# Expert weights in eight double slots of 2 MB instead of sixteen slots of 1 MB

## The chip, the cores and the metric

The kernel runs on one core of one Trainium2 chip. The metric is the device time of one execution in microseconds (us); lower is better. A difference of about 0.2% (2.8 us) is what a measurement of this kernel can tell from no change.

## The reference

One layer over 256 tokens of width 1024, all in float32. Three token mixers (a gated linear recurrence, a chunked mLSTM, a chunked gated delta rule) share one projection, are gated, summed and projected, and a layer norm follows. Then comes a mixture of 32 experts, of which each token uses four, and a second layer norm. The change touches the expert part alone:

```python
logits = (xf @ router_w + router_b).astype(jnp.float32)
top_val, top_idx = lax.top_k(logits, TOP_K)          # TOP_K = 4 of N_EXPERTS = 32
gate = jax.nn.softmax(top_val, axis=-1)
...
def expert_block(args):
    tok, e = args
    hdn = x_pad[tok] @ w1[e] + b1[e]                 # w1[e]: 1024 x 2048
    glu, lin = hdn[:, :D_FF], hdn[:, D_FF:]
    glu = jnp.minimum(glu, SWIGLU_LIMIT)
    lin = jnp.clip(lin, -SWIGLU_LIMIT, SWIGLU_LIMIT)
    act = glu * jax.nn.sigmoid(SWIGLU_ALPHA * glu) * (lin + 1.0)
    return act @ w2[e] + b2[e]                       # w2[e]: 1024 x 1024
...
x = layer_norm(DN_ALPHA * x + y, ln2_g[l], ln2_b[l])
```

Every expert's weights are read once: 32 experts of 12 MB, 384 MB in all.

## The kernel before, in words

The kernel has two stages. The first, about a third of the time, computes the mixers, the output projection, the first layer norm and the routing. Its weights come in tiles of up to 1 MB (rows of 1 KB) through three buffers; line 377 issues each when the tile three places ahead has been used (`full`, line 338). The end of that stream is, in this order: `br20`, `ga22`, `br21`, `ga23`, `br22`, `br23`, `wo0` to `wo3` (`ga` and `wo` tiles are 1 MB, these `br` tiles 0.5 MB).

The second stage walks over the experts in 16 pairs. One pair's weights are laid out in 24 chunks of 1 MB: 16 for the up projection (8 input blocks for each half `f` of the hidden width) and 8 for the down projection. A chunk is 128 partitions by 2048 floats, so a row of 8 KB for each partition, and holds both experts of the pair side by side. `pair` (line 795) issues for every chunk eight matmuls of 512 columns: `up` at line 818, `down` at line 836. Between chunks stand the biases (line 811), the scatter of the pair before into the accumulators (`scatter`, line 763), the gather of the next pair's tokens (`gather`, line 775), the gates (line 854) and the turning of the hidden values (line 827). At the end of a pair ScalarE copies the result out (line 1145), and the next pair's `scatter` adds it in. After the last pair a last `scatter`, the second layer norm and two stores follow.

The chunks live in 16 slots of 8 KB for each partition: 12 in `ring`, 4 in `mix` (`SLOT`, line 308). SyncE issues all loads, one after the other, in `load_chunk` (line 357). Each slot has a semaphore `chunk_in<slot>`, on which `chunk(c)` makes the tensor engine wait; the last matmul of a chunk raises `chunk_used`. `load_turn` (line 399) issues chunk n when chunk n - 16 has been used (the wait is at line 402). The first 16 chunks have no such wait: four go out between the last mixer weights (after `br20`, `ga22`, `br21`, `ga23`), eight right after `wo3`, and slots 12 to 15 after the last output projection (`wo11` full for two, moved for one) and after the second router product (`lgt1` full for the last).

Of the kernel before, what the change touches and what calls it, by code (L numbers as in the profile page):

```python
# [18 lines left out]
P = 128  # L19
S = 256  # L20
NT = S // P
D = 1024
# [8 lines left out]
NE, TOPK, FF = 32, 4, 1024  # L31
KF = FF // P
NPAIR = NE // 2
EC = 2 * KD + KF
SLOTS = 16
RSLOTS = 12
PB = 2
CAP = 64
ROUNDS = S // CAP
# [149 lines left out]
def layer_kernel(nc, x, w_in, lru_conv_w, lru_conv_b, lru_wa, lru_ba, lru_wx, lru_bx,  # L189
# [3 lines left out]
    uses, bank_total = bank_uses()  # L193
    stream = weight_stream()
    stream_at = {name: n for n, (name, _, _) in enumerate(stream)}

    def stream_value(n):

        return 16 * sum(2 if src == "lru" else 1 for _, src, _ in stream[n % WBUFS:n + 1:WBUFS])
# [3 lines left out]
    with ExitStack() as ctx:  # L203
        sems = {}

        def E(name):

            if name not in sems:
                sems[name] = ctx.enter_context(nc.semaphore("s_" + name))
            return sems[name]  # L210

        RING = ctx.enter_context(nc.sbuf_tensor("ring", [P, 96 * 256], F32))
        MIX = ctx.enter_context(nc.sbuf_tensor("mix", [P, 28400], F32))
# [3 lines left out]
        def area(base, kb, words):  # L217
            return base[:, int(kb * 256):int(kb * 256) + words]
# [86 lines left out]
        B1R = area(MIX, 72.25, 512)  # L305


        SLOT = [area(RING, 8 * n, 2048) for n in range(RSLOTS)] + [area(MIX, kb, 2048)
                                                                   for kb in (48.25, 56.25, 24, 32)]

        XE = [area(MIX, 4 * n, KD * P).rearrange("p (c n) -> p c n", c=KD) for n in range(PB)]
        GLU = area(MIX, 8, 512)
# [25 lines left out]
        def full(eng, name):  # L338

            bank, n = uses[name]  # L340
            eng.wait_ge(E(f"bank_full{bank}"), n)

        def moved(eng, name):

            bank, n = uses[name]
            eng.wait_ge(E(f"bank_free{bank}"), n)
# [4 lines left out]

        @block.sync
        def _(sp):
            def load_chunk(n, pair):

                src = expert_w[bass.ds(pair, 1), n % EC].rearrange("e p n -> p (e n)")
                sp.dma_start(SLOT[n % SLOTS], src).then_inc(E(f"chunk_in{n % SLOTS}"), 16)  # L357


            ahead = [stream_at[name] for name in ("br20", "ga22", "br21", "ga23")]  # L360
            for t in range(NT):
                sp.dma_start(XTOK[:, t, :], x[0, t * P:(t + 1) * P, :]).then_inc(E(f"x_in{t}"), 16)
            for n, (name, src, col) in enumerate(stream):
                buf, loaded = WB[n % WBUFS], E(f"w_in{n % WBUFS}")
                if name == "wo3":
                    buf, loaded = WO3, E("wo3_in")
                    full(sp, "br03")
                elif n >= WBUFS:
                    full(sp, stream[n - WBUFS][0])
                if src == "lru":  # L370
                    both = buf.rearrange("p c n -> p (c n)").rearrange("p (k b n) -> p k b n", k=2, b=NB)
                    sp.dma_start(both[:, 0], lru_wa[0].rearrange("b i j -> i b j")).then_inc(loaded, 16)
                    sp.dma_start(both[:, 1], lru_wx[0].rearrange("b i j -> i b j")).then_inc(loaded, 16)
                    continue
                w = sources[src][0]
                k = w.shape[0] // P
                sp.dma_start(buf[:, 0:k, :], w[:, col:col + GW].rearrange("(c p) n -> p c n", p=P)
                             ).then_inc(loaded, 16)
                if name == "gq1":

                    sp.wait_ge(E("small_zero"), 4)
                    for q, (first, cols) in enumerate(((C_MI, MH), (C_MI + MH, MH), (C_GA, GH), (C_GA + GH, GH))):
                        sp.dma_start(WSM[:, :, 32 * q:32 * q + cols], w_in[0, :, first:first + cols]
                                      .rearrange("(c p) n -> p c n", p=P)).then_inc(E("wsm_in"), 16)
                if n == ahead[0]:
                    for event in ("ha_ready", "hb_ready", "hc_ready"):
                        sp.wait_ge(E(event), 1)
                if n in ahead:
                    load_chunk(ahead.index(n), 0)
            for n in range(len(ahead), RSLOTS):  # L390
                load_chunk(n, 0)
            full(sp, "wo11")
            load_chunk(RSLOTS, 0)
            load_chunk(RSLOTS + 1, 0)
            moved(sp, "wo11")
            load_chunk(RSLOTS + 2, 0)
            full(sp, "lgt1")
            load_chunk(RSLOTS + 3, 0)
            def load_turn(turn, pair, first=0):

                for n in range(first, PB * EC):
                    sp.wait_ge(E("chunk_used"), turn * PB * EC + n - SLOTS + 1)
                    load_chunk(n, pair + n // EC)
            load_turn(0, 0, SLOTS)
            with sp.Fori(1, NPAIR // PB) as q:
                load_turn(q, q * PB)
            sp.wait_ge(E("rounds_ready"), 1)
            rounds = sp.value_load(NR[0:1, 0:1], min_val=1, max_val=ROUNDS)
            with sp.If(rounds > 1):
                with sp.Fori(1, rounds) as r:  # L410
                    with sp.Fori(0, NPAIR // PB) as q:
                        load_turn(r * (NPAIR // PB) + q, q * PB)
            for t in range(NT):
                sp.wait_ge(E("out_ready"), t + 1)
                sp.dma_start(out[0, t * P:(t + 1) * P, :], X1[:, t, :]).then_inc(E("stored"), 16)
            sp.wait_ge(E("stored"), 16 * NT)
# [30 lines left out]
        def _(pe):  # L447
# [349 lines left out]
            def pair(turn, j):  # L797
# [4 lines left out]
                def chunk(c):  # L802

                    n = j * EC + c
                    pe.wait_ge(E(f"chunk_in{n % SLOTS}"), 16 * (PB * EC // SLOTS) * turn + 16 * (n // SLOTS) + 16)
                    return SLOT[n % SLOTS]

                def bias(f, bank):
                    for g in range(2):
# [4 lines left out]
                def up(f, c, bank):  # L814
                    w = chunk(f * KD + c)
                    for g in range(2):
                        for a in range(2):
                            ins = mm(PS[64 * a:64 * a + 64, bank + g, :], XE[j][:, c, 64 * a:64 * a + 64],  # L818
                                     w[:, a * D + g * 512:a * D + g * 512 + 512], start=False, stop=(c == KD - 1),
                                     skip_group_check=True)  # L820
                    ins.then_inc(E("chunk_used"), 1)
# [10 lines left out]
                def down(c, bank):  # L832
                    w = chunk(2 * KD + c)
                    for h in range(2):
                        for a in range(2):
                            ins = mm(PS[64 * a:64 * a + 64, bank + h, :], HT[:, c // 4, c % 4, 64 * a:64 * a + 64],  # L836
                                     w[:, a * D + h * 512:a * D + h * 512 + 512], start=(c == 0), stop=(c == KF - 1),
                                     skip_group_check=True)
                    ins.then_inc(E("chunk_used"), 1)
# [842 lines left out]

def expert_layout(w1, w2, b1):

    up = w1[0].reshape(NPAIR, 2, KD, P, 2, 2, 512).transpose(0, 5, 2, 3, 1, 4, 6).reshape(NPAIR, 2 * KD, P, 2 * D)
    down = w2[0].reshape(NPAIR, 2, KF, P, D).transpose(0, 2, 3, 1, 4).reshape(NPAIR, KF, P, 2 * D)
    return np.concatenate([up, down], 1), b1[0].reshape(NE, 4, 512).transpose(1, 0, 2).reshape(4 * NE, 512)


# [17 lines left out]
```

## Time and profile before

| | us |
|---|---|
| median of 3 runs (1422.99 to 1423.6) | 1423.18 |
| the profiled execution | 1421.26 |
| its span, first to last instruction | 1419.5 |
| TensorE busy (share of the span) | 1347.7 (95%) |
| VectorE, ScalarE, GpSimd busy | 358.6, 181.8, 7.4 |
| moved by DMA | 458.42 MB, 323 GB/s over the span |

The profile covers one execution. Times in it count from its first instruction. Its page divides the span into 40 slices of 35.5 us and shows for each how busy the engines and the 16 DMA engines were. MB and GB/s in the profile are decimal; an expert chunk is 1,048,576 bytes. TensorE's busy time counts pipelined matmuls and does not tell by itself that TensorE is the limit. "SPq" is SyncE's instruction queue, where DMAs are issued; a duration there is the time until the issuing instruction was done, not the transfer's.

### The profile page before, as it was taken

How to read it: one execution, taken by the hardware profiler on the slowest of the kernel's cores; microseconds unless marked ns; L12 is line 12 of the kernel's file. 1: busy time of each engine (PE TensorE's matmuls, PEld its weight loads, DVE VectorE, ACT ScalarE, POOL GpSimd, SP SyncE). 2: the span in 40 equal slices, each digit the busy share in tenths (PEclk: the TensorE clock that was granted, in tenths of full speed). 3: DMA queues.
4: the chain of work that ended last, by engine and by line, in shares of the span. 5: the costliest groups of instructions: out<-in, count | busy, mean ns of one | idle time of the engine just before them, and what ended most of it. 6: DMA issues, size and time to landing. Idle time of an engine off the chain costs nothing.

```text
span 1419.5 us, 19162 instructions
## 1 busy us (share of the span) xinstructions
PE 1347.7 (95%) x7864; PEld 749.0 (53%) x7864; DVE 358.6 (25%) x738; ACT 181.8 (13%) x278; POOL 7.4 (1%) x19
## 2 busy tenths in 40 slices
PE   8999999999999999999999899898999989999895
PEld 7889889988888534434434233332333324333241
DVE  4845667212114220120120110201102011120103
ACT  1331251101100200100100010010010001001000
POOL 1000000000000000000000000000000000000000
PEclk9999999999999999999999999999999999999999
DMA  7433222233579799999999999999999999999995
GB/s 216 148 119 89 60 90 60 90 118 104 178 269 365 261 411 421 421 421 422 422 422 422 422 422 422 422 422 422 422 422 422 422 422 422 422 422 422 422 422 215
DMA packets 112530, 458.42 MB, mean 323 GB/s; under 512 B 12633, under 2 KB 62029, under 8 KB 63341
## 3 DMA queue, kind: packets, MB, share of 16 engines
q1 hardware_dynamic: 110016, 454.16, 80.2%
q10 hardware_dynamic: 2476, 3.75, 0.8%
q8 instruction: 26, 0.43, 0.1%
q14 instruction: 12, 0.09, 0.0%
HBM read 456.83 MB, written 1.05 MB: 323 GB/s over the span
## 4 chain that ended last, share of the span: by engine, by line
PE 51%; DMA 24%; SPq 20%; DVE 3%; issue 2%; ACT 0%; DVEq 0%
SPq L357 20%; PE ps L471 19%; DMA ring<-expert_w 19%; PE ps L818 10%; PE ps L489 6%; PE ps L836 6%; DMA mix<-expert_w 4%; PE ps L775 2%; PE ps L763 2%; PE ps L811 2%; PE ps L710 1%; PE ps L481 1%; DMA mix<-w_out 1%; DMA mix<-w_in 1%; PE ps L827 0%
## 5 line engine op out<-in xcount | busy, mean ns | idle before, releaser
L818 PE MATMUL ps<-ring,mix 128*64 128x512 f32 x1536 | 343.1, 592 | 2.4 <-DMA ring<-expert_w 2.4
L471 PE MATMUL ps<-mix 128*128 128x256 f32 x1280 | 281.5, 380 | 1.0 <-DMA mix<-w_in 1.0
L471 PEld LDWEIGHTS ps<-mix 128*128 128x128 f32 x1280 | 241.5, 190 | 35.2 <-issue 2.9
L818 PEld LDWEIGHTS ps<-ring,mix 128*64 128x64 f32 x1536 | 108.6, 137 | 210.3 <-issue 192.5
L836 PE MATMUL ps<-ring,mix 128*64 128x512 f32 x768 | 181.4, 599 | 31.4 <-DMA ring<-expert_w 31.3
L1645 DVE TENSOR_SCALAR mix<-ps 128x512 f32<-128x512 f32 x32 | 22.1, 692 | 539.5 <-PE ps L818 539.5
L836 PEld LDWEIGHTS ps<-ring,mix 128*64 128x64 f32 x768 | 50.4, 136 | 149.1 <-issue 83.1
L818 PE MATMUL ps<-mix 128*64 128x512 f32 x512 | 116.4, 593 | 2.0 <-DMA mix<-expert_w 2.0
L1654 DVE COPY mix<-ps 128x512 f32<-128x512 f32 x32 | 22.1, 692 | 239.2 <-PE ps L827 239.2
L836 PE MATMUL ps<-mix 128*64 128x512 f32 x256 | 60.6, 601 | 12.5 <-DMA mix<-expert_w 12.5
L818 PEld LDWEIGHTS ps<-mix 128*64 128x64 f32 x512 | 35.2, 137 | 63.3 <-issue 53.7
L775 PEld LDWEIGHTS ps<-mix 128*64 128x64 f32 x1088 | 61.9, 138 | 11.0 <-issue 9.1
L775 PE MATMUL ps<-mix 128*64 128x128 f32 x1088 | 65.9, 275 | 0.5 <-DVEq L1630 0.5
L1143 ACT ACTIVATE mix<-mix 128x512 f32<-128x512 f32 x32 | 20.2, 630 | 332.2 <-DVE mix L1645 332.2
L489 PE MATMUL ps<-ring 128*128 128x128 f32 (+2 forms) x512 | 62.6, 281 | 0.0
L763 PE MATMUL ps<-mix 128*64 128x512 f32 x272 | 61.3, 592 | 1.1 <-ACT mix L1145 1.1
L489 PEld LDWEIGHTS ps<-ring 128*128 128x128 f32 x512 | 61.3, 192 | 1.3
L811 PE MATMUL ps<-mix 128*64 128x512 f32 x256 | 60.4, 592 | 0.0
L1145 ACT COPY mix<-ps 128x1024 f32<-128x1024 f32 x16 | 16.2, 1012 | 274.1 <-PE ps L836 274.1
L836 PEld LDWEIGHTS ps<-mix 128*64 128x64 f32 x256 | 16.8, 136 | 55.9 <-issue 30.8
L763 PEld LDWEIGHTS ps<-mix 128*64 128x64 f32 x272 | 19.4, 137 | 40.3 <-issue 38.3
L827 PEld LDWEIGHTS ps<-mix 128*64 128x64 f32 x512 | 30.2, 137 | 18.3 <-issue 18.3
(252 smaller groups left out, 779.7 us busy)
## 6 DMA issues: line engine op xcount, KB each, us to landing
ring<-expert_w SPq DMA_DIRECT2D x288, 1024.0 KB, 26.4
mix<-expert_w SPq DMA_DIRECT2D x96, 1024.0 KB, 27.4
mix<-w_in SPq DMA_DIRECT2D x34, 1024.0 KB, 5.3
mix<-w_br_lru SPq DMA_DIRECT2D x4, 1024.0 KB, 5.2
mix<-w_out SPq DMA_DIRECT2D x4, 1024.0 KB, 5.7
mix<-w_br_ml SPq DMA_DIRECT2D x4, 512.0 KB, 3.4
mix<-w_br_gd SPq DMA_DIRECT2D x4, 512.0 KB, 5.4
mix<-x SPq DMA_DIRECT2D x2, 512.0 KB, 5.5
```

Of the source, the lines that this page charges most:

```text
L357: sp.dma_start(SLOT[n % SLOTS], src).then_inc(E(f"chunk_in{n % SLOTS}"), 16)
L471: ins = mm(o[:, m * S:(m + 1) * S], w[:, c, m * P:(m + 1) * P], rhs[:, c, :], start=(m == 0 and c == 0), stop=(c == nk - 1), skip_group_ch ...
L489: ins = mm(o[0:lhs.shape[-1], lo:hi], lhs, rhs, start=True, stop=True, skip_group_check=True)
L763: ins = mm(PS[64 * a:64 * a + 64, 4 + 2 * t + h, :], GTS[:, t * P + 64 * a:t * P + 64 * a + 64], YS[:, h * 512:(h + 1) * 512], start=False ...
L775: ins = mm(PS[64 * a:64 * a + 64, bank, c * P:(c + 1) * P], X1[:, t, k:k + 64], ONE[:, t, :], start=(c == 0 and t == 0), stop=(t == NT - 1 ...
L811: mm(PS[64 * a:64 * a + 64, bank + g, :], PICK[:, 2 * g + f, a, :], B1R, start=True, stop=False, skip_group_check=True)
L818: ins = mm(PS[64 * a:64 * a + 64, bank + g, :], XE[j][:, c, 64 * a:64 * a + 64], w[:, a * D + g * 512:a * D + g * 512 + 512], start=False, ...
L827: ins = mm(PS[64 * a:64 * a + 64, bank, c * P:(c + 1) * P], HID[:, c * P + 64 * a:c * P + 64 * a + 64], ident, start=True, stop=True, skip ...
L836: ins = mm(PS[64 * a:64 * a + 64, bank + h, :], HT[:, c // 4, c % 4, 64 * a:64 * a + 64], w[:, a * D + h * 512:a * D + h * 512 + 512], sta ...
L1143: A(SIG, GLU, ACT.Sigmoid, scale=SWIGLU).then_inc(E("sig_ready"), 1)
L1645: ts(GLU, PS[:, bank, :], LIMIT, None, ALU.min).then_inc(E("glu_ready"), 1)
L1654: nc_v.tensor_copy(HT[:, n[1], :, :], PS[:, bank, :].rearrange("p (q n) -> p q n", q=4)).then_inc(E("ht_ready"), 1)
```

## The change

The 24 chunks of a pair are laid out in DRAM as 12 steps of two: a step is 128 partitions by 4096 floats, a row of 16 KB for each partition, in which the two chunks stand behind each other. One DMA of 2 MB loads a step. There are eight slots of 16 KB for each partition in the same memory: six in `ring`, and two in `mix` that lie where the four single ones lay. One semaphore belongs to each double slot. TensorE waits for a step at each of its two chunks and reads its half of the slot. SyncE issues step n when both chunks of step n - 8 have been used. Of the first eight steps, one goes out after `br20`, one after `br21`, four after `wo3`, one when `wo11` is full, and the last when `lgt1` is full. All arithmetic stays as it was.

```diff
+STEPS = 2
-SLOTS = 16
-RSLOTS = 12
+SLOTS = 8
+RSLOTS = 6
...
-        SLOT = [area(RING, 8 * n, 2048) for n in range(RSLOTS)] + [area(MIX, kb, 2048)
-                                                                   for kb in (48.25, 56.25, 24, 32)]
+        SLOT = [area(RING, 16 * n, 4096) for n in range(RSLOTS)] + [area(MIX, kb, 4096) for kb in (48.25, 24)]
...
-            def load_chunk(n, pair):
-
-                src = expert_w[bass.ds(pair, 1), n % EC].rearrange("e p n -> p (e n)")
-                sp.dma_start(SLOT[n % SLOTS], src).then_inc(E(f"chunk_in{n % SLOTS}"), 16)
+            def load_steps(n, pair):
+
+                src = expert_w[bass.ds(pair, 1), n % (EC // STEPS)].rearrange("e p n -> p (e n)")
+                sp.dma_start(SLOT[n % SLOTS], src).then_inc(E(f"steps_in{n % SLOTS}"), 16)
...
-                if n in ahead:
-                    load_chunk(ahead.index(n), 0)
-            for n in range(len(ahead), RSLOTS):
-                load_chunk(n, 0)
+                if n in ahead[::STEPS]:
+                    load_steps(ahead.index(n) // STEPS, 0)
+            for n in range(len(ahead) // STEPS, RSLOTS):
+                load_steps(n, 0)
             full(sp, "wo11")
-            load_chunk(RSLOTS, 0)
-            load_chunk(RSLOTS + 1, 0)
+            load_steps(RSLOTS, 0)
             moved(sp, "wo11")
-            load_chunk(RSLOTS + 2, 0)
             full(sp, "lgt1")
-            load_chunk(RSLOTS + 3, 0)
+            load_steps(RSLOTS + 1, 0)
             def load_turn(turn, pair, first=0):
 
-                for n in range(first, PB * EC):
-                    sp.wait_ge(E("chunk_used"), turn * PB * EC + n - SLOTS + 1)
-                    load_chunk(n, pair + n // EC)
+                for n in range(first, PB * EC // STEPS):
+                    sp.wait_ge(E("chunk_used"), turn * PB * EC + STEPS * (n - SLOTS + 1))
+                    load_steps(n, pair + n // (EC // STEPS))
...
-                    pe.wait_ge(E(f"chunk_in{n % SLOTS}"), 16 * (PB * EC // SLOTS) * turn + 16 * (n // SLOTS) + 16)
-                    return SLOT[n % SLOTS]
+                    m = n // STEPS
+                    pe.wait_ge(E(f"steps_in{m % SLOTS}"),
+                               16 * (PB * EC // STEPS // SLOTS) * turn + 16 * (m // SLOTS) + 16)
+                    return SLOT[m % SLOTS][:, 2 * D * (n % STEPS):2 * D * (n % STEPS + 1)]
...
-    return np.concatenate([up, down], 1), b1[0].reshape(NE, 4, 512).transpose(1, 0, 2).reshape(4 * NE, 512)
+    steps = np.concatenate([up, down], 1).reshape(NPAIR, EC // STEPS, STEPS, P, 2 * D).transpose(0, 1, 3, 2, 4)
+    return (steps.reshape(NPAIR, EC // STEPS, P, STEPS * 2 * D),
+            b1[0].reshape(NE, 4, 512).transpose(1, 0, 2).reshape(4 * NE, 512))
```

## Rows read from the trace of the kernel before

**Rows 1.** The page, part 2: DMA engines, busy tenths and GB/s in 40 slices; packets.
```profile
DMA  7433222233579799999999999999999999999995
GB/s 216 148 119 89 60 90 60 90 118 104 178 269 365 261 411 421 421 421 422 422 422 422 422 422 422 422 422 422 422 422 422 422 422 422 422 422 422 422 422 215
DMA packets 112530, 458.42 MB, mean 323 GB/s; under 512 B 12633, under 2 KB 62029, under 8 KB 63341
```

**Rows 2.** Lines of TensorE: 500 to 690 us, then 900 to 1300 us (busy, mean | idle before).
```profile
L836 PE MATMUL ps<-ring,mix 128*64 128x512 f32 x192 | 42.6, 592 | 0.0
...
L836 PE MATMUL ps<-ring,mix 128*64 128x512 f32 x320 | 77.1, 602 | 17.7 <-DMA ring<-expert_w 17.7
```

**Rows 3.** Chain, in order of time (start us, us, what), late in the stream.
```profile
1124.41 26.45 DMA ring<-expert_w
...
1153.58 5.99 SPq L357
...
1184.06 26.45 DMA ring<-expert_w
```

**Rows 4.** Windows: us, busy of PE, PEld, DVE, ACT, POOL, PEclk, DMA share, GB/s.
```profile
422.25:423.25 1.00, 1.00 (x6) 0.89 (x5) 0.57 (x1) 0.00 (x0) 0.00 (x0) 1.00 1.09 389
459.00:462.00 3.00, 1.72 (x13) 1.23 (x12) 2.54 (x9) 0.03 (x1) 0.00 (x0) 1.00 1.01 426
505.00:510.00 5.00, 5.00 (x30) 1.86 (x28) 0.00 (x0) 0.00 (x0) 0.00 (x0) 1.00 1.01 428
900.00:1000.00 100.00, 91.73 (x540) 34.43 (x540) 14.54 (x34) 8.40 (x11) 0.00 (x0) 1.00 1.01 422
```

**Rows 5.** DMA view, the one issue at 478.5 us, its time to landing alone.
```profile
ring<-expert_w SPq DMA_DIRECT2D x1, 1024.0 KB, 5.6
```

**Rows 6.** Timeline of SyncE's queue, 477 to 506 us: the first refills of the slots.
```profile
478.50 2.04 SPq L357 DMA_DIRECT2D ring<-expert_w  x2
...
485.37 2.04 SPq L357 DMA_DIRECT2D ring<-expert_w  x2
...
490.99 0.33 SPq L357 DMA_DIRECT2D ring<-expert_w  x1
...
494.45 3.76 SPq L357 DMA_DIRECT2D ring<-expert_w  x3
...
501.32 3.76 SPq L357 DMA_DIRECT2D ring<-expert_w  x3
```

**Rows 7.** Windows: the gap before the first refill and the stretch behind it.
```profile
472.00:479.00 7.00, 7.00 (x50) 3.17 (x48) 1.65 (x8) 2.35 (x4) 0.00 (x0) 1.00 0.01 2
479.50:500.00 20.50, 20.50 (x152) 9.53 (x150) 1.98 (x3) 3.46 (x5) 0.00 (x0) 1.00 0.89 321
```

**Rows 8.** Chain at the end: the last chunk's matmuls and the copy behind them.
```profile
1402.03 1.96 PE ps L836 x8
...
1404.01 1.02 ACT mix L1145
```

**Rows 9.** Timeline of SyncE's queue, 384 to 420 us: mixer weights and first chunks.
```profile
385.18 0.42 SPq L357 DMA_DIRECT2D ring<-expert_w  x1
391.59 0.37 SPq L377 DMA_DIRECT2D mix<-w_in  x1
...
401.95 0.37 SPq L377 DMA_DIRECT2D mix<-w_in  x1
408.86 3.82 SPq L377 DMA_DIRECT2D mix<-w_br_gd  x2
```

**Rows 10.** DMA view of the issues at 391.6 and 401.9 us: times to landing.
```profile
mix<-w_in SPq DMA_DIRECT2D x1, 1024.0 KB, 10.0
...
mix<-w_in SPq DMA_DIRECT2D x1, 1024.0 KB, 9.4
```

**Rows 11.** Chain, the first pair and the begin of the second, on TensorE.
```profile
474.88 1.87 PE ps L811 x8
...
520.19 8.58 PE ps L836 x40
528.77 1.72 PE ps L811 x8
```

## The prediction

> **What bounds the kernel now.** I read the slices first. The DMA engines are nine tenths busy or more from the fifteenth slice to the last but one, and from the sixteenth at 421 or 422 GB/s without a dent [rows 1]. So the question is whether TensorE waits for them. The lines view answers by stretch: from 500 to 690 us the down projection (line 836) never waits, in the 400 us from 900 it idles 17.7 us for `ring<-expert_w` [rows 2]. TensorE begins with a full set of slots, uses it up until about 700 us, and from then on runs at the pace of the stream. In the chain the same link comes back every 59.65 us (1184.06 - 1124.41), which is one pair, 24 chunks, so 2.485 us a chunk [rows 3]. A million bytes and a bit (1,048,576) in 2.485 us is 422 GB/s, the rate of the slices: nothing but the transfers sets this pace. The chain's pieces on "SPq L357", such as 5.99 us [rows 3], are the issuing instruction held up behind a full queue. They cost nothing, for the DMA share stays at 1.01 meanwhile [rows 4].
>
> So the end is: the moment from which the stream no longer pauses, plus the chunks left times the time of one, plus what follows the last landing. The change works on all three.
>
> **The rate of the stream.** A transfer of 128 rows over 16 engines gives each engine eight rows. At 1 KB rows the saturated rate is 389 GB/s [rows 4]; an engine moves a sixteenth of it, so a row takes 1024 / 24.3 = 42.1 ns. At 8 KB rows the best stretches reach 426 to 428 GB/s [rows 4]; at 427, an engine's 65,536 bytes of a chunk take 2456 ns. Let each row cost a fixed f besides its bytes, and the hand-over to the next transfer about the same f. Then 2456 = 9f + 64 x (42.1 - f), so f = 238 / 55 = 4.3 ns. A step of two chunks with 16 KB rows needs nine f where two chunks needed eighteen: 9 x 4.3 = 39 ns less, of 4970.
>
> In the long stretch a chunk takes 2485 ns, 29 ns more than in the best ones. No row tells whether this extra goes with the bytes (it stays, 58 ns a step) or with the rows (half goes, another 29 ns). The ends are a saving of 39 and of 68 ns a step. I take the middle, 53 ns, and keep both ends.
>
> How many steps count? 384 chunks less the 16 preloaded and the 8 of the start below: 360 chunks, 180 steps. The saving is 180 x 53 ns = 9.6 us, between 7.0 and 12.2.
>
> Here the Trainium skill speaks twice. A lone chunk takes 5.6 us to land [rows 5] but 2.485 us in the stream [rows 3]: the fixed part of a transfer lies beside other transfers. The Trainium skill, SBUF — State Buffer, section "The DMA setup-cost knee", says that each transfer pays roughly 2 us whatever its size. Read as serial cost it would give 192 transfers fewer, some 380 us; the trace disagrees, since nearly nothing of it is left in the stream. The Trainium skill, DMA: Bandwidth & Descriptors, section "Why small descriptors are slow", gives about 3 cycles a packet (3.5 ns at the 850 MHz stated there), where the rows give 4.3; by its figure the certain part of the saving is 180 x 9 x 3.5 ns = 5.7 us, an estimate, instead of 7.0.
>
> **The start: the first refills.** With all 16 chunks landed the DMA engines stand still from 472 to 479 us [rows 7] until TensorE has used a chunk. SyncE's queue shows the refills: 478.50 and 480.22 (two issues, 1.72 apart, the time of eight matmuls), 485.37 and 487.09, 490.99, 494.45 and 496.17 and 497.88, then 501.32 [rows 6]. Served one after the other at 2.49 us each they end at 480.99, 483.48, 487.86, 490.35, 493.48, 496.94, 499.43, 501.92 (all later by the same latency, which cancels); the next is there at 501.32, so no pause follows. A step goes out at the second of each two: 480.22, 487.09, 494.45, 497.88. At 4.97 us they end at 485.19, 492.06, 499.42, 504.39, and the next is issued at 503.04, in time. The stream falls into its steady run 2.5 us later. My sum draws the pauses of before somewhat too long (3.5 us, where a share of 0.89 against 1.01 over 20.5 us makes 2.4 [rows 7]), so 1.5 to 2.5 us; I take 2.5. TensorE does not wait for this: it holds 16 chunks until 700 us. But the stream never pauses again, so nothing gives the 2.5 us back.
>
> **The end.** Before, the last chunk's eight matmuls follow its landing at once: 1.96 us, then the copy at line 1145 [rows 8]. Now both chunks of the last step land together, and the last but one also runs after the landing. Chunks back to back take 8.58 / 5 = 1.72 us [rows 11]. That is +1.7 us. In the middle of the run it costs nothing, as two chunks (3.7 us) fit into the 4.97 us to the next step.
>
> **The mixers' end.** The second chunk now goes in front of `ga22` instead of behind it, and the fourth in front of `ga23`. `ga22` is issued at 391.59 and lands 10.0 us later, at 401.6 [rows 9, 10]; TensorE turns to it when `ga23` goes out, 401.95, the moment at which `br20` has been used. Only 0.35 us is spare. A chunk issued at 385.18 is through by about 390, so the double one ends around 392.7, just as `ga22` (391.6 plus about 1 us) begins to move: a delay of 0 to 0.3 us, under cover. `ga23` lands at 401.95 + 9.4 = 411.35; TensorE needs it at 412.3, when the last `br` tile of the pair at 408.86 goes out [rows 9]. In front of it stand the same bytes as before, two chunks. I cost both at nothing; if the cover fails, TensorE is the bound there and up to 0.5 us goes straight into the end. Slot 14's load moves from the moved `wo11` to the full `lgt1`, some 8 us later, but the engines stand idle at 472 us with everything landed [rows 7], and the chunk is used after 505 us. Nothing.
>
> **Edits with one answer.** Half the issues on SyncE: it is never what the stream waits for. Fewer descriptors: the queue was held up at 26.45 us from issue to landing [rows 3], some 10.6 chunks; eight steps stay within 16 MB, seven of which are under way or landed while one is used, and TensorE falls behind by at most the work between a pair's chunks, 53.9 - 24 x 1.72 = 12.6 us [rows 11], under three steps. The stream doesn't starve. TensorE's instructions are the same.
>
> **Sum.** -9.6 + 2.5 + 1.7 = -5.4 us, between -8.0 and -2.8, or -3.8 with the small start. The profiled execution took 1421.26, 1.8 over its span and 1.9 under the median of 1423.18; the change adds nothing outside the span, so the difference is set against the median: 1417.8.
>
> **Rivals.**
> *The extra vanishes.* The rate with 16 KB rows stays at its undisturbed best all along: 39 + 58 = 97 ns a step, -17.5 + 4.2 = -13.3 us, 1409.9. For it: whole stretches run at 428 [rows 4]. Against: they are short, and with a deep queue every slice reads 422 [rows 1]. 5%.
> *Nothing gained (just slower).* The change doesn't do what it says: the queue cuts a 16 KB row into two pieces, or the fixed 4.3 ns of a 1 KB row isn't there at 8 KB. Then at most the hand-over, 180 x 4.3 ns = 0.8 us, is saved, and the coarser grain costs its 4.2: +3.4 us, 1426.6. For it: no transfer of before has rows over 8 KB. 20%.
> *Longer rows collide more (slower).* The engines' rows lie twice as far apart in DRAM, 16 KB instead of 8. If the 29 ns extra a chunk is engines getting in each other's way, and it doubles for the same bytes, a step costs 58 - 39 = 19 ns more: +3.4 + 4.2 = +7.6 us, 1430.8. It decides from the point at which a step takes more than 4970 - 4200 / 180 = 4947 ns; every further 1% is 8.9 us. For it: the extra comes up with a deep queue; against: 8 KB rows suffer only 1.2%. 12%. [...]
> *A new wait at the mixers' end* eats the gain: 3%.
>
> **Chances.** The forecast has 60%, of which 12 points lie at the end where the extra stays, within 0.2%. 0.2% of 1423 is 2.8 us, about what a measurement of this kernel can tell from no change. Faster: 48 + 5 = 53%. Within: 12, 9 of the 20 of nothing gained (3.4 us is just past the line), and 3: 24%. Slower: 11 + 12 = 23%. The range runs from 1410 to 1428: it takes in both ends of the forecast and nothing gained, and leaves out most of the collisions and half of the vanishing extra. The forecast's own range is 1415.2 to 1420.4.
>
> **What the profile would show.** Packets fall from 112,530 [rows 1] by some 24,600 for the rows and 3,000 for the hand-overs, if rows aren't cut. The slices from the sixteenth on read 424 to 428 GB/s instead of 422, if the rate gains, and the chain comes back after 59.0 to 59.2 us. The first refill is issued near 480.2. At the end 16 matmuls of line 836 stand behind the last landing. No new idle before line 471 between 385 and 425 us. I am wrong if the slices read 422 or less, or if the start of the second stage moves.

## The result and the profile after

The changed kernel takes 1411.85 us (median of 4 runs, 1410.07 to 1414.87); the kernel before, on the same chips, 1423.39. The ratio is 0.9924, with a 95% interval of 0.9912 to 0.9936: 11.5 us faster, where 5.4 was forecast. The profiled execution took 1411.46 us, its span is 1409.7, 9.8 us less than before.

From the page of the changed kernel, part 2 as in [rows 1]:

```profile
DMA  7433121232579699999999999999999999999994
GB/s 217 149 120 90 60 90 61 90 119 90 171 272 354 242 399 427 428 428 430 428 429 429 427 430 428 429 429 427 429 429 429 428 428 430 428 428 429 427 430 200
DMA packets 84879, 458.39 MB, mean 325 GB/s; under 512 B 9560, under 2 KB 58956, under 8 KB 60268
```

The slices read 427 to 430 GB/s where they read 421 or 422. The packets are 27,651 fewer: the 24,576 rows and 3072 hand-overs that vanish if a 16 KB row goes in one piece, and three others. The page's DMA list gives 33.1 us for the landing of a 2 MB step in `ring`, from issue on; nothing waits for that number, as with the 26.4 us of before.

The chain late in the stream (start us, us, what), beside [rows 3]:

```profile
829.91 32.08 DMA ring<-expert_w
...
1064.86 32.05 DMA ring<-expert_w
...
1123.60 32.02 DMA mix<-expert_w
...
1182.30 32.02 DMA ring<-expert_w
```

The link now comes back once a pair, in turn in `ring` and in `mix`. Single links are 58.70 to 58.77 us apart; the six pairs from 829.91 to 1182.30 us take 352.39 us, 58.73 a pair, 4.894 us a step. Three pairs of before, from this link to the last of [rows 3], take 178.91 us, 59.64 a pair, 4.970 for the same bytes:

```profile
1005.15 26.44 DMA ring<-expert_w
```

TensorE still waits for the stream, in the same place as before (lines view, 900 to 1300 us, beside [rows 2]): the bound has not changed, only its pace.

```profile
L836 PE MATMUL ps<-ring,mix 128*64 128x512 f32 x320 | 74.3, 598 | 22.2 <-DMA ring<-expert_w 22.2
```

Where the 9.8 us of the span lie is read from two links of the chain: the first matmuls of the second stage and the copy after the last chunk. The first line stands in the stretch 472 to 482 us, the others at the end.

```profile
475.98 1.87 PE ps L811 x8
...
1358.45 32.04 DMA mix<-expert_w
...
1390.54 3.68 PE ps L836 x16
...
1394.24 1.02 ACT mix L1145
```

Before, these two stand at 474.88 and 1404.01 [rows 11, rows 8]. So the second stage, from its first bias matmul to the last copy, took 929.13 us and takes 918.26: 10.9 us less. It began 1.1 us later, and behind the copy both need the same 15.5 us. The start of the second stage moves from run to run for a reason of its own (below), so this length of the second stage is the sharper measure. It comes from one trace of each kernel; the changed kernel was profiled a second time, with 918.41 us.

### The profile page after: what moved, and what is told of

Same layout as the page of the kernel before. It is cut to its first block, busy times and chain, and to the rows that moved or that the text cites. A ratio compares the mean times of both kernels' runs of the same rounds, so it can differ in the third digit from the quotient of the medians.

```text
span 1409.7 us, 18467 instructions
## 1 busy us (share of the span) xinstructions
PE 1338.6 (95%) x7864; PEld 756.4 (54%) x7864; DVE 358.3 (25%) x738; ACT 181.8 (13%) x278; POOL 7.4 (1%) x19
## 4 chain that ended last, share of the span: by engine, by line
PE 68%; DMA 29%; DVE 3%; issue 0%; SPq 0%; ACT 0%; DVEq 0%
PE ps L818 20%; PE ps L469 19%; DMA mix<-expert_w 14%; DMA ring<-expert_w 14%; PE ps L836 7%; PE ps L487 6%; PE ps L773 4%; PE ps L761 4%; PE ps L811 2%; PE ps L708 1%; PE ps L479 1%; DMA mix<-w_out 1%; DMA mix<-w_in 1%; PE ps L854 0%; PE ps L827 0%
## 5 line engine op out<-in xcount | busy, mean ns | idle before, releaser
L818 PE MATMUL ps<-ring,mix 128*64 128x512 f32 x1536 | 341.9, 592 | 0.0
L818 PEld LDWEIGHTS ps<-ring,mix 128*64 128x64 f32 x1536 | 109.2, 137 | 205.8 <-issue 199.4
L836 PE MATMUL ps<-ring,mix 128*64 128x512 f32 x768 | 176.1, 596 | 38.0 <-DMA ring<-expert_w 38.0
L836 PEld LDWEIGHTS ps<-ring,mix 128*64 128x64 f32 x768 | 53.9, 137 | 146.9 <-issue 98.8
L818 PE MATMUL ps<-mix 128*64 128x512 f32 x512 | 115.4, 592 | 0.0
L773 PEld LDWEIGHTS ps<-mix 128*64 128x64 f32 x1088 | 62.7, 140 | 10.8 <-issue 9.1
L818 PEld LDWEIGHTS ps<-mix 128*64 128x64 f32 x512 | 35.7, 137 | 59.6 <-issue 57.9
L836 PE MATMUL ps<-mix 128*64 128x512 f32 x256 | 57.9, 596 | 9.6 <-DMA mix<-expert_w 9.6
L761 PE MATMUL ps<-mix 128*64 128x512 f32 x272 | 61.3, 592 | 1.1 <-ACT mix L1145 1.1
L811 PE MATMUL ps<-mix 128*64 128x512 f32 x256 | 60.4, 592 | 0.0
L836 PEld LDWEIGHTS ps<-mix 128*64 128x64 f32 x256 | 18.5, 137 | 48.7 <-issue 36.5
L761 PEld LDWEIGHTS ps<-mix 128*64 128x64 f32 x272 | 19.5, 137 | 40.2 <-issue 38.2
L827 PEld LDWEIGHTS ps<-mix 128*64 128x64 f32 x512 | 30.1, 137 | 18.3 <-issue 18.3
## 6 DMA issues: line engine op xcount, KB each, us to landing
ring<-expert_w SPq DMA_DIRECT2D x144, 2048.0 KB, 33.1
```

Of the source, the lines that this page charges most:

```text
L761: ins = mm(PS[64 * a:64 * a + 64, 4 + 2 * t + h, :], GTS[:, t * P + 64 * a:t * P + 64 * a + 64], YS[:, h * 512:(h + 1) * 512], start=False ...
L773: ins = mm(PS[64 * a:64 * a + 64, bank, c * P:(c + 1) * P], X1[:, t, k:k + 64], ONE[:, t, :], start=(c == 0 and t == 0), stop=(t == NT - 1 ...
L811: mm(PS[64 * a:64 * a + 64, bank + g, :], PICK[:, 2 * g + f, a, :], B1R, start=True, stop=False, skip_group_check=True)
L827: ins = mm(PS[64 * a:64 * a + 64, bank, c * P:(c + 1) * P], HID[:, c * P + 64 * a:c * P + 64 * a + 64], ident, start=True, stop=True, skip ...
```

## The experiments

Theory "rows": each row of a transfer costs an engine a fixed time besides its bytes; the change halves the rows. Rivals: "transfers" (half as many transfers and hand-overs, and a queue that no longer fills), "place" (the rows' spacing in DRAM), and the depth of the queue.

**Undo the rows alone: 2 MB transfers with 8 KB rows.** Slots, waits and the number of transfers are those of the changed kernel; the data lie in DRAM as before.

```diff
-                src = expert_w[bass.ds(pair, 1), n % (EC // STEPS)].rearrange("e p n -> p (e n)")
-                sp.dma_start(SLOT[n % SLOTS], src).then_inc(E(f"steps_in{n % SLOTS}"), 16)
+                c = STEPS * (n % (EC // STEPS))
+                src = expert_w[bass.ds(pair, 1), c:c + STEPS].rearrange("e k p n -> p (e k) n")
+                sp.dma_start(SLOT[n % SLOTS].rearrange("p (k n) -> p k n", k=STEPS), src).then_inc(E(f"steps_in{n % SLOTS}"), 16)
...
```

The part left out (...) is the layout function, here and in the next two experiments.

> The changed kernel with one thing undone: its 2 MB transfers and double slots stay, but each transfer is made of rows of 8 KB (two pieces for each partition, out of the chunk layout of before). Theory 'rows': the gain is a cost that every row pays besides its bytes, some 8 ns (4 undisturbed and 4 of the extra seen with a deep queue), so with 8 KB rows the stream is back at 422 to 423 GB/s, a pair takes 59.6 us, only the coarser grain is left, and the time is 3 to 5 us over the kernel before: 1426 to 1428 us. Theory 'transfers': the gain comes from half as many transfers, hand-overs and issues and a queue that no longer fills, so the stream stays at 429 GB/s and the time at 1411 to 1413 us.

Measured: 1426.40 us, ratio to before 1.0026 (1.0016 to 1.0037). Its chain, late in the stream, and the two ends of its second stage:

```profile
477.74 1.87 PE ps L812 x8
...
1134.77 32.96 DMA mix<-expert_w
...
1254.06 32.95 DMA mix<-expert_w
...
1409.98 1.02 ACT mix L1146
```

Two pairs take 119.29 us, 59.645 each: the pace of before (59.64) to the hundredth, though there are half as many transfers. So "transfers" falls, and with it my own term for the hand-over. What is left is the price of the coarse grain: a second stage of 932.24 us, 3.1 more than before. Against the changed kernel, from which it differs by its rows alone, it is 13.98 us longer. That is 76 ns (4.970 - 4.894 us) for each of the 184 steps that are not preloaded.

**Undo the place alone: the kernel before, out of the new layout.** 1 MB transfers, 8 KB rows, but 16 KB apart in DRAM.

```diff
-                src = expert_w[bass.ds(pair, 1), n % EC].rearrange("e p n -> p (e n)")
+                c = n % EC
+                src = expert_w[bass.ds(pair, 1), c // 2, :, 2 * D * (c % 2):2 * D * (c % 2 + 1)
+                               ].rearrange("e p n -> p (e n)")
...
```

> The kernel before (1 MB transfers, rows of 8 KB, sixteen slots), but its weights lie in DRAM as in the changed kernel, so that the 8 KB rows of a transfer are 16 KB apart. Theory 'rows': where the rows lie doesn't matter, 422 GB/s, 1423 us. Theory 'place': the wider spacing is what changes how the engines meet in DRAM; if it is what helped, 429 GB/s and 1409 us; if it hurts, below 422 GB/s and over 1426 us.

Measured: 1422.44 us, ratio 1.0002 (0.9993 to 1.0012).

```profile
476.57 1.87 PE ps L813 x8
...
1125.56 26.44 DMA ring<-expert_w
...
1185.19 26.44 DMA ring<-expert_w
...
1405.33 1.02 ACT mix L1147
```

The two links shown are 59.63 us apart, and the second stage takes 928.76 us. The wider spacing neither helps nor hurts.

**Halve the rows the other way: 4 KB.** The kernel before, each chunk laid out as two halves.

```diff
-                src = expert_w[bass.ds(pair, 1), n % EC].rearrange("e p n -> p (e n)")
-                sp.dma_start(SLOT[n % SLOTS], src).then_inc(E(f"chunk_in{n % SLOTS}"), 16)
+                src = expert_w[bass.ds(pair, 1), n % EC].rearrange("e h p n -> p (e h) n")
+                sp.dma_start(SLOT[n % SLOTS].rearrange("p (h n) -> p h n", h=2), src).then_inc(E(f"chunk_in{n % SLOTS}"), 16)
...
```

> The kernel before with rows of 4 KB: same 1 MB transfers and slots, each partition's 8 KB in two pieces that lie apart in DRAM. Theory 'rows', all of it by rows: a chunk takes 16 rows of 150.6 + 8.3 ns and a hand-over, 2548 ns for 2485, 411 to 412 GB/s, about 23 us more: 1446 us. If only the undisturbed 4.3 ns goes by rows and the deep-queue extra by bytes: 2517 ns, 417 GB/s, 12 us more: 1435 us. Theory 'transfers': no change, 1423 us.

Measured: 1449.82 us, ratio 1.0193 (1.0176 to 1.0211), 27.4 us over before on its chip.

```profile
1041.75 20.75 DMA mix<-expert_w
...
1287.51 20.75 DMA mix<-expert_w
```

Four pairs in 245.76 us make 2.560 us a chunk, 75 ns more for 8 rows more: 9.3 ns a row. That is over even the upper of my two expectations (8.3 ns): the fixed cost and with it the 29 ns that I had called the "extra" of the long stretch go by rows.

**Is the extra the queue's depth? At most three chunks in flight.** The kernel before, with its loads written out (the loop's own edit is left out here):

```diff
                     sp.wait_ge(E("chunk_used"), turn * PB * EC + n - SLOTS + 1)
+                    if shallow:
+                        m = turn * PB * EC + n - 3
+                        sp.wait_ge(E(f"chunk_in{m % SLOTS}"), 16 * (m // SLOTS) + 16)
```

> The kernel before, but SyncE issues chunk n only when chunk n - 3 has landed, so that at most three chunks are under way (loads written out instead of looped, so that this wait is on constants). It asks where the extra 29 ns a chunk of the long stretch comes from. If from the deep queue or its being held up: 426 to 428 GB/s as in the short best stretches, 9 to 11 us less than before, 1412 to 1414 us, and the depth, no longer rows alone, has to be named for part of the gain. If from anything else (rows, engines out of step): 422 GB/s and 1422 to 1424 us.

Measured: 1426.39 us, ratio 1.0028 (1.0019 to 1.0038). Chain, and the window from 900 to 1000 us (columns as in [rows 4]):

```profile
1204.08 7.39 DMA ring<-expert_w
...
1211.54 7.38 DMA ring<-expert_w
...
900.00:1000.00 100.00, 91.20 (x512) 32.86 (x510) 14.53 (x34) 8.03 (x10) 0.00 (x0) 1.00 1.01 420
```

Three chunks take 7.46 us, 2.487 each, with three in the queue as with ten. From ten down to three, depth is not the cause; fewer than three were not tried. The kernel is even 4 us slower than before (second stage 932.98 us), which neither theory had: single stretches fall below 422 GB/s while the DMA share stays at 1.01, so these are no pauses. What they are I have not found.

**The next size: 32 KB rows.** Steps of four chunks in three slots. The scatter inside the pairs is left out, as the expectation says, so only the rate counts.

```diff
-STEPS = 2
-SLOTS = 8
-RSLOTS = 6
+STEPS = 4
+SLOTS = 3
+RSLOTS = 3
...
-        SLOT = [area(RING, 16 * n, 4096) for n in range(RSLOTS)] + [area(MIX, kb, 4096) for kb in (48.25, 24)]
+        SLOT = [area(RING, 32 * n, 8192) for n in range(RSLOTS)]
...
-                scatter(None)
```

> Rows of 32 KB: steps of four chunks, 4 MB, into three slots of 32 KB for each partition (ring only), all three preloaded after the last mixer weights. So that three slots suffice, the scatter inside the pairs is left out (line 763 in the loop: the contributions of all pairs but the last are missing from the result). Only the rate counts. Chunk times so far: 2.560 us with 4 KB rows, 2.485 with 8 KB, 2.446 with 16 KB, that is 9.3 and 9.8 ns for each row saved on an engine. Theory 'every row costs 9.5 ns, bytes go at 2409 ns a chunk': 2409 + 2 x 9.5 = 2.428 us a chunk, 58.3 us a pair, 432 GB/s. If rows over 16 KB are cut, or another cost appears, a pair stays at 58.7 us and 429 GB/s or gets slower.

Measured: 1419.49 us. The chain has (the two lines are four pairs apart):

```profile
1043.88 20.87 DMA ring<-expert_w
...
1277.01 20.88 DMA ring<-expert_w
```

Four pairs in 233.13 us, 58.28 a pair, 2.428 us a chunk: what the law of the other sizes gave (58.3). The 2.446 us and 9.8 ns in the expectation came from a single link of 58.70 us; over six pairs a chunk takes 2.447 us and a row 9.5 ns. Two constants now give four sizes, one of them forecast:

| row | us a pair | ns a chunk | 2409 ns + rows x 9.5 ns |
|---|---|---|---|
| 4 KB | 61.44 | 2560 | 2561 |
| 8 KB | 59.64 | 2485 | 2485 |
| 16 KB | 58.73 | 2447 | 2447 |
| 32 KB | 58.28 | 2428 | 2428 |

In time this kernel lies behind the changed one all the same, even without its scatter: its refills begin late, as a slot comes free only after four chunks, and four chunks (7.10 us) stand behind the last landing.

**Make the coarse places fine.** Two kernels on top of the changed one: the last step of every two pairs as two halves, and the same with the first four refills in halves too. The edit of the second is shown; the first lacks its two blocks on the first four refills.

```diff
+            def load_half(n, pair, h, event):
+
+                a = 2 * D * h
+                src = expert_w[bass.ds(pair, 1), n % (EC // STEPS), :, a:a + 2 * D].rearrange("e p n -> p (e n)")
+                sp.dma_start(SLOT[n % SLOTS][:, a:a + 2 * D], src).then_inc(E(event), 16)
...
                 for n in range(first, PB * EC // STEPS):
+                    if first and n < first + 4:
+                        for h, event in enumerate((f"steps_in{n % SLOTS}", f"half_in{n % SLOTS}")):
+                            sp.wait_ge(E("chunk_used"), STEPS * (n - SLOTS) + h + 1)
+                            load_half(n, pair + n // (EC // STEPS), h, event)
+                        continue
                     sp.wait_ge(E("chunk_used"), turn * PB * EC + STEPS * (n - SLOTS + 1))
+                    if n == PB * EC // STEPS - 1:
+                        load_half(n, pair + 1, 0, f"steps_in{n % SLOTS}")
+                        load_half(n, pair + 1, 1, "last_in")
+                        continue
...
+                    if SLOTS <= m < SLOTS + 4 and n % STEPS:
+                        pe.wait_ge(E(f"half_in{m % SLOTS}"), 16)
+                    if n == PB * EC - 1:
+                        pe.wait_ge(E("last_in"), 16 * turn + 16)
```

> The changed kernel with its two coarse places made fine: the first four refills go out as eight halves of 1 MB, each when one chunk has been used, with a semaphore of their own for the second halves; and the last step of every two pairs is loaded as two halves. My costs of the coarser grain are 2.5 us at the first refills and 1.7 us behind the last landing. If they are right, this kernel wins 3.5 to 4 us over the changed one, 1407.5 to 1409 us beside 1411.9, with 8 matmuls instead of 16 of line 836 behind the last landing and the steady stream unchanged at 429 GB/s. If the stream has slack somewhere that swallows a later start (rival), only the 1.7 us of the end shows, about 1410 us.

> As the run with halves at both ends, but only the last step of every two pairs is loaded as two halves; the first refills stay at 2 MB. By my costs 1.7 us less than the changed kernel less 0.3 us for the shorter rows: 1410 to 1411 us, and the kernel with halves at both ends another 2.5 us below. If the first refills cost nothing, both kernels with halves take the same time.

> The changed kernel itself on the same chip, as the measure for the two kernels with halves: 0.992 of the kernel before, about 1411.5 us.

Measured on one chip (ratios to the kernel before): the changed kernel again 1412.48 us, 0.9927 (0.9914 to 0.9941); last step in halves 1411.28, 0.9924 (0.9911 to 0.9938); both ends 1411.91, 0.9927 (0.9914 to 0.9941). I had forecast up to 4 us between them. The whole times don't tell them apart; the second stage does. The ends of the stage, for the changed kernel again, the last step in halves, and both ends in halves:

```profile
477.41 1.87 PE ps L811 x8
...
1392.12 3.68 PE ps L836 x16
...
1395.82 1.02 ACT mix L1145
```

```profile
477.07 1.87 PE ps L823 x8
...
1387.74 7.10 PE ps L848 x32
...
1394.87 1.02 ACT mix L1157
```

```profile
477.20 1.87 PE ps L830 x8
...
1386.12 7.10 PE ps L855 x32
...
1393.25 1.02 ACT mix L1164
```

The stage takes 918.41, 917.80 and 916.05 us, one trace each. The halves at the start give 1.75 us. The halves at the end give 0.6. Behind the landing named by the chain, now that of the last step but one, TensorE runs four chunks without a pause (7.10 us) and not the eight matmuls I had expected: the last half is no longer waited for. From that landing to the copy it is 7.3 us; in the changed kernel it is 8.6 (4.9 to the next landing, 3.7 behind it), so this end gains 1.4 us. The other side is the shorter rows of one step in every two pairs, by the law 8 x 9.5 = 76 ns in each of eight turns, 0.6 us. In the version with the last step in halves two pairs take 117.54 us, where twice 58.73 makes 117.46:

```profile
1130.47 31.86 DMA ring<-expert_w
...
1248.01 31.87 DMA ring<-expert_w
```

The version with halves at both ends has the shortest second stage of all, 2.4 us less than the changed kernel; in whole times, spread over 2 us, that does not show.

## Why the prediction was right, and where its sizes were off

The direction and the mechanism came as forecast, the size did not: 1411.85 us lies outside the forecast's own range of 1415.2 to 1420.4. The wide range from 1410 takes it in only because its lower end had been stretched towards a rival, "the extra vanishes", whose reason does not hold.

**The bound and the three places**: right. The sum with the measured terms is -180 x 76 ns = -13.7, +1.75, +1.7: -10.2 us, against the 10.9 us that the second stage is shorter. With the small start the fast end of my sum is -12.2 + 1.5 + 1.7 = -9.0 us and not the -8.0 that I gave; 1414.2 us does not reach the measured time either.

**The rate of the stream**: the term that was mis-sized. I took 53 ns a step, between 39 and 68; it is 76. Both readings under it were of windows too short for what I took from them. First, the undisturbed rate of 426 to 428 GB/s. Windows of 5 us scatter: from 900 to 1000 us, in an even stream, twenty of them read 419 to 426 GB/s before and 423 to 439 after. Right behind the pause, where I had read 428 over 5 us, 50 us read 422, the rate of the long stretch (kernel before, then the changed one for the last line; columns as in [rows 4]):

```profile
505.00:555.00 50.00, 50.00 (x314) 20.59 (x312) 8.61 (x19) 3.82 (x6) 0.00 (x0) 1.00 1.01 422
510.00:515.00 5.00, 5.00 (x36) 2.14 (x34) 1.48 (x3) 0.06 (x1) 0.00 (x0) 1.00 1.01 421
940.00:945.00 5.00, 5.00 (x62) 3.35 (x60) 0.00 (x0) 1.16 (x2) 0.00 (x0) 1.00 1.02 426
925.00:930.00 5.00, 5.00 (x26) 1.72 (x24) 0.00 (x0) 1.75 (x2) 0.00 (x0) 1.00 1.03 439
```

So no stretch of the traces shows a faster stream. The 29 ns a chunk that I shared between rows and bytes are no cost of their own, and the run with three chunks in flight looked for the cause of something that these traces don't have. Second, the 389 GB/s for 1 KB rows is a single microsecond with a DMA share of 1.09; the microseconds from 421 and from 423 us read 331 and 259, with shares of 0.98. The law of the four sizes would give a chunk of 1 KB rows 2409 + 64 x 9.5 = 3017 ns, 348 GB/s, an estimate; no run has a long stretch of such rows. The 4.3 ns a row that I worked out from the two readings are less than half of the 9.5 ns that the four sizes show; 8 rows less at 9.5 ns make the 76 ns.

The hand-over, for which I had charged another 4.3 ns, costs nothing that the run with 2 MB and 8 KB rows shows. The fixed time of a transfer (the Trainium skill, SBUF — State Buffer, "The DMA setup-cost knee", roughly 2 us) was rightly set aside: between that run and the kernel before, 12 transfers a pair less change the pair by less than 0.02 us. The 3 cycles a packet of the Trainium skill, DMA: Bandwidth & Descriptors, "Why small descriptors are slow", 3.5 ns, fall short too: a row costs 9.5 ns here.

**The first refills**: right in kind, 2.5 us forecast, 1.75 measured. I had named the 1.5 as the lower end, since my sum drew the pauses of before too long. The changed kernel's queue shows them as I had placed them, 6.9, 14.2 and 17.7 us after the first (SyncE's queue, three stretches):

```profile
481.32 0.33 SPq L357 DMA_DIRECT2D ring<-expert_w  x1
...
488.19 0.33 SPq L357 DMA_DIRECT2D ring<-expert_w  x1
...
495.55 3.76 SPq L357 DMA_DIRECT2D ring<-expert_w  x2
```

**The end**: right. From the start of the last matmuls to the copy 1.98 us before [rows 8] and 3.70 after. The whole price of the coarse grain, 2.5 + 1.7 = 4.2 (or 3.2 with the small start), is 3.1 us against the kernel before and 3.5 against its twin in the new layout.

**The mixers' end**: right. `ga22` lands after 10.1 us (10.0 before [rows 10]), and TensorE runs from 383.77 to 425.93 us without a gap.

**The start of the second stage** moved by 1.1 us, which I had named as a sign against me. It isn't the change. Windows of the changed kernel (columns as in [rows 4]):

```profile
466.00:468.00 2.00, 1.99 (x6) 1.35 (x6) 1.35 (x7) 0.00 (x0) 0.00 (x0) 0.50 1.14 475
468.00:470.00 2.00, 1.93 (x12) 1.00 (x12) 1.57 (x11) 0.00 (x0) 0.00 (x0) 0.50 0.95 410
470.00:472.00 2.00, 2.00 (x22) 2.00 (x20) 0.69 (x6) 0.00 (x0) 0.00 (x0) 0.50 0.94 401
```

The same windows of the kernel before:

```profile
466.00:468.00 2.00, 1.87 (x6) 0.74 (x6) 1.68 (x10) 0.00 (x0) 0.00 (x0) 0.77 1.02 356
468.00:470.00 2.00, 1.50 (x13) 1.30 (x14) 1.57 (x12) 0.00 (x0) 0.00 (x0) 0.50 1.00 385
470.00:472.00 2.00, 2.00 (x36) 2.00 (x34) 0.69 (x5) 0.43 (x1) 0.00 (x0) 0.88 0.39 164
```

The granted clock stands at half, 1.2 GHz, in all three after the change, and for a part of the windows on both sides (0.90 and 0.89): 6.8 us in all. Before it was 0.77, 0.50 and 0.88, with 1.00 on both sides: 3.4 us. The 3.4 us more at half the clock are worth up to 1.7 us, an estimate from these windows. TensorE had idled in short pieces for VectorE's routing in the 7 us up to the drop, 1.3 and 0.8 us, but in both kernels alike, so why the drop lasts longer in one than in the other is not shown. The same program moves as well: the changed kernel starts its second stage at 475.98 in one trace and at 477.41 in the other, and the kernel before in the new layout, whose stream has the old pace, at 476.57. Over all runs the start lies between 474.88 and 477.74 us. The clock is a part of this only: with 2 MB transfers and 8 KB rows TensorE began the sixteen matmuls of line 488 at 462.55 us; the same sixteen (line 489) began at 460.78 before, and the clock had not dropped yet in either. All of it shifts the whole second stage by up to 3 us and explains a part of the spread of the times.

**The rivals**: "nothing gained" is out by the packet count and the run with 2 MB and 8 KB rows; "collide" by the run with the wide spacing; "the extra vanishes" came near the time (-13.3) for a wrong reason: there was no extra to vanish, each row costs the same 9.5 ns, on half as many rows.

**What stays open**: what in a row costs the 9.5 ns, and why the run with three chunks in flight is 4 us slower.

## What to carry to other kernels

A stream of full-width loads that never pauses pays by bytes and by rows: here 2409 ns for 1,048,576 bytes (435 GB/s if rows cost nothing) and 9.5 ns for each row on an engine. Doubling rows from 8 to 16 KB gave 1.5%, and the next doubling gave 0.8% of the stream's pace, in a kernel that lost more than that at its two ends. The number of transfers doesn't matter while the queue is full; it matters at the two ends, where a larger transfer starts later and leaves more work behind its landing. Read a rate from a stretch of tens of us or from links several rounds apart, not from the best window of a few us. When the start of a stage wanders from run to run, compare the stage's own length by two links of the chain.

## What the runs showed that I had not expected

The fixed cost follows the number of rows over a factor of eight in their length to within 1 ns a chunk. Halving the number of transfers at equal rows left the pace at 59.645 us a pair against 59.64. And the part before the second stage, the same on TensorE in all these programs, ends up to 3 us earlier or later, in part by how long TensorE's clock stays at 1.2 GHz around 467 us: 3.4 or 6.8 us.
